# The last down projection with its tokens on the partitions

## The reference

```python
def squared_relu_mlp(h, w1, w2):
    return jnp.square(jax.nn.relu(h @ w1)) @ w2
...
        x = x + squared_relu_mlp(rms_norm_2(x, norm_mlp[layer]), mlp_w1[layer], mlp_w2[layer])
...
    return rms_norm_2(x, final_norm)
```

## Time and profile before

| what | us |
|---|---|
| median of three runs | 1201.18 |
| the three runs | 1198.7, 1201.18, 1201.41 |
| profiled execution, span from first to last instruction | 1197.3 |
| PE busy | 1187.6 (99%) |
| VectorE busy | 867.8 (72%) |
| ScalarE busy | 646.7 (54%) |
| GpSimd busy | 220.6 (18%) |

### The profile page before, as it was taken

One profiled execution on the slowest core, in us unless ns is written; L12 is line 12 of the kernel. 1 busy time (PEld: TensorE's weight loads), 2 busy tenths in 40 slices (PEclk: granted clock), 3 DMA queues, 4 the chain that ended last, 5 costly groups with the idle time before them and its releaser, 6 DMA issues.

```text
span 1197.3 us, 19531 instructions
## 1 busy us (share of the span) xinstructions
PE 1187.6 (99%) x7802; PEld 1060.7 (89%) x7802; DVE 867.8 (72%) x1199; ACT 646.7 (54%) x868; POOL 220.6 (18%) x110
## 2 busy tenths in 40 slices
PE   9999999999999999999999999999999999999997
PEld 6888889988899888888999988888899878888886
DVE  6877767788868877766788786655579777766553
ACT  6655554465654755545643555543446784555441
POOL 0443301000000344310000025510000340554000
PEclk9999999999999999999999999999999999999999
DMA  8655555953345555555545555555576305555540
GB/s 315 213 178 195 191 177 182 285 201 107 106 150 181 179 204 179 200 186 189 177 160 179 193 199 203 179 206 177 192 265 246 107 2 178 209 181 205 179 174 36
DMA packets 31569, 217.53 MB, mean 182 GB/s; under 512 B 3584, under 2 KB 3856, under 8 KB 6272
## 3 DMA queue, kind: packets, MB, share of 16 engines
q1 hardware_dynamic: 30000, 210.33, 50.4%
q0 software_dynamic: 1344, 5.53, 1.6%
q10 hardware_dynamic: 144, 0.52, 0.1%
HBM read 215.30 MB, written 4.22 MB: 183 GB/s over the span
## 4 chain that ended last, share of the span: by engine, by line
PE 96%; DVE 2%; ACT 1%; DMA 1%; issue 0%; POOL 0%; DVEq 0%; ACTq 0%; SPq 0%; POOLq 0%
PE bank L1564 42%; PE bank L1565 21%; PE bank L1557 8%; PE bank L1558 7%; PE bank L1559 7%; PE bank L1965 1%; PE bank L1673 1%; DVE w_hl L816 1%; PE bank L1737 1%; PE bank L1675 1%; PE bank L1674 1%; DMA raw<-weights 1%; ACT w_hl L418 0%; PE bank L1859 0%; PE bank L1842 0%; PE bank L1878 0%
## 5 line engine op out<-in xcount | busy, mean ns | idle before, releaser
L816 DVE TENSOR_TENSOR w_hl<-raw,w_hl 128x2048 fp32r<-128x2048 f32 x194 | 444.1, 2289 | 116.5 <-ACT w_hl L418 115.5
L418 ACT ACTIVATE w_hl<-raw 128x2048 fp32r<-128x2048 f32 x195 | 370.6, 1903 | 113.8 <-PE bank L1565 65.5
L1564 PE MATMUL bank<-x_hl,w_hl 128*128 128x512 f32 x908 | 316.5, 395 | 0.0
L1564 PE MATMUL bank<-hidden,w_hl 128*128 128x512 f32 x832 | 288.6, 394 | 0.0
L369 POOL TENSOR_TENSOR hidden<-hid_f,hidden 128x256 fp32r<-128x256 f32 (+1 forms) x76 | 189.5, 2493 | 519.8 <-ACT hidden L501 307.0
L1565 PE MATMUL bank<-x_hl,w_hl 128*128 128x256 f32 x908 | 251.9, 277 | 0.0
L1565 PE MATMUL bank<-hidden,w_hl 128*128 128x256 f32 x832 | 230.5, 277 | 0.0
L1564 PEld LDWEIGHTS bank<-x_hl,w_hl 128*128 128x128 f32 x908 | 170.3, 188 | 39.6
L1564 PEld LDWEIGHTS bank<-hidden,w_hl 128*128 128x128 f32 x832 | 156.0, 188 | 36.2
L1565 PEld LDWEIGHTS bank<-x_hl,w_hl 128*128 128x128 f32 x908 | 170.6, 188 | 0.1
L479 ACT ACTIVATE second<-bank 128x512 f32<-128x512 f32 (+1 forms) x107 | 57.2, 535 | 199.1 <-PE bank L1565 199.0
(11 more groups left out here) (385 smaller groups left out, 1536.0 us busy)
## 6 DMA issues: line engine op xcount, KB each, us to landing
raw<-weights SPq DMA_DIRECT2D x197, 1024.0 KB, 4.9
bias_skew<-bias_rows POOLq DMA_DIRECT2D x1, 3072.0 KB, 26.0
gate_or_bias<-bias_skew POOLq DMA_DIRECT2D x1, 2048.0 KB, 9.6
h<-x_t SPq DMA_DIRECT2D x2, 512.0 KB, 6.0
out_t<-out_g SPq DMA_DIRECT2D x4, 256.0 KB, 2.5
con<-consts SPq DMA_DIRECT2D x1, 769.5 KB, 13.3
raw<-weights ACTq DMA_DIRECT2D x1, 512.0 KB, 5.2
raw<-weights SPq DMA_DIRECT2D x1, 512.0 KB, 7.9
```

What stands on the lines that cost most here:

```text
L418: nc.scalar.activation(dst, src, ACT.Copy).then_inc(hi_split, 1)
L816: V.tensor_tensor(w_lo[:, s, :], raw[:, s, :], w_hi[:, s, :].bitcast(F32), ALU.subtract).then_inc(lo_split, 1)
L1564: mm(out_, w_hi[:, s, c:c + m], x, start=start, stop=False, **kw)
```

## The change

The down projection of "mlp1" is turned round. Its weights are packed as 2 x 8 chunks, each 512 hidden features by half of the 1024 output columns (`HALF`), and a new `last_down` takes the place of the second part of `feed_forward` on PE: for each half, chunk and tile of 128 tokens, four hidden tiles of 128 tokens are stationary in turn and 512 columns of weights move. The sums of a half lie in two banks, one per token tile (6 and 7, then 0 and 1). In the last half the final two chunks are taken for all of the first token tile before the second. Behind the first chunk PE transposes `h` (16 pieces) into banks 0 to 3 and `t_b` (two) into bank 4; ScalarE copies `h` out as `h_tok`, VectorE the factor as `r_tok`.

The rest then works on token rows: one VectorE operation per bank updates `h_tok`; ScalarE squares it and sums along the row in the same instruction; the mean, Ln, Exp and Newton step are taken per token tile; the factor is a scalar of each partition. The final gain, before a column of `par`, is loaded by GpSimd's queue into all partitions (`gain_b`, in place of `sv`). GpSimd multiplies three of the four quarters by the gain and the whole first token tile by its factor, VectorE and ScalarE take one half of the second tile each. Three stores leave from SP, SP and ScalarE, as rows of `out`, and the host no longer transposes. The matmuls against ones and zeros and the spreading of the factors at the end go. Cut to its core:

```diff
-            downs("mlp1", "final", None)
+            last_down()
...
+                nxt(c0)
+                act.wait_ge(tok_mm, 1)
+                for n in range(4):
+                    nc.scalar.activation(half_of(h_tok[:, n // 2, :], n % 2), bank[:, n, :], ACT.Copy).then_inc(tok_in, 1)
+                for i in range(1, FC):
+                    nxt(c0 + i)
...
+                    nc.scalar.activation(sq_flat[:, HALF * n:HALF * n + HALF], half_of(h_tok[:, n % 2, :], n // 2), ACT.Square,
+                                         accum_out=f_ss[:, n:n + 1]).then_inc(f_sq, 1)
...
+                y = half_of(out_g[:, 1, :], 0)
+                nc.scalar.activation(y, y, ACT.Copy, scale=f_r[:, 1:2]).then_inc(y_act, 1)
+                act.wait_ge(y_act, 1)
+                act.dma_start(out[P:2 * P, 0:HALF], y).then_inc(stored, 16)
...
+                V.scalar_tensor_tensor(out=hj, in0=bank[:, LAST_BANKS[half] + t, :], scalar=r_tok[:, 0, t:t + 1], in1=hj,
+                                       op0=ALU.mult, op1=ALU.add).then_inc(f_upd, 1)
...
+            dve.wait_ge(f_r_ready, 2)
+            V.tensor_scalar(y, y, f_r[:, 1:2], None, ALU.mult).then_inc(y_dve, 1)
...
+                order = [(half, i, t) for half in range(2) for i in range(FC - 2 * half) for t in range(2)]
+                order += [(1, i, t) for t in range(2) for i in (FC - 2, FC - 1)]
...
+                        mm(o, a, wh, start=f == 0, stop=False)
+                        mm(o, a, wl, start=False, stop=False)
+                        ins = mm(o, l, wh, start=False, stop=f == 2 * MF - 1)
...
+                        pe.wait_ge(ab_ready, b + MF)
+                        pe.wait_ge(h_upd, UPD["mlp1"])
+                        for n in range(2):
+                            for k in range(KT):
+                                nc.tensor.transpose(bank[:, 2 * n + k // 4, k % 4 * P:k % 4 * P + P], h[:, k, P * n:P * n + P], ident)
...
+            pool.wait_ge(phi_mm, 1)
+            pool.dma_start(gain_b, last_gain.partition_broadcast(P)).then_inc(last_gain_in, 16)
             low("mlp1")
...
+            pool.wait_ge(f_r_ready, 1)
+            nc.gpsimd.tensor_tensor(out_g[:, 0, :], out_g[:, 0, :], f_r[:, 0:1].to_broadcast([P, D]),
+                                    ALU.mult).then_inc(y_pool, 1)
```

More of the change, by code:

```diff
@@ L140, in done, with program @@
         self.wait()
-def program(nc, x_t, p_t, positions, weights, small, consts, rel_bias, bias_rows, bias_skew, out):
+def program(nc, x_t, p_t, positions, weights, small, consts, rel_bias, last_gain, bias_rows, bias_skew, out):
     with ExitStack() as ctx:
@@ L528, in downs @@
                     if used and o == KT - 1:
                         nxt(c)
[L530 to L539, removed]
+                rsqrt(following, load=stage in ("ffn1", "ffn2"))
@@ L955, in downs @@
                     if ended:
[L956 to L963, removed]
+                        dve.wait_ge(second_out, SECOND[stage] + UPS[stage] + o + 1)
+                        st.done(V.tensor_tensor(t_ab[:, 0, :], bank[:, DOWN_BANKS[o], 0:S], second[:, o % 2, 0, :], ALU.add))
+                        st.done(V.tensor_tensor(t_ab[:, 1, :], t_ab[:, 0, :], factor_of[:, :], ALU.mult))
                         V.scalar_tensor_tensor(out=h[:, o, :], in0=t_ab[:, 1, :], scalar=scale, in1=h[:, o, :],
@@ L1533, in _ @@
             factor("mlp1")
-            st.done(V.tensor_tensor(t_b[:, :], r_sb[:, :], r_sb[:, :], ALU.mult))
+            V.tensor_tensor(t_b[:, :], r_sb[:, :], r_sb[:, :], ALU.mult).then_inc(r_ready, 1)
+            dve.wait_ge(r_ready, 3)
             ups("mlp1")
-            downs("mlp1", 1.0, "final", None, None)
-            dve.wait_ge(ss_ready, NO["final"] + 1)
-            V.tensor_scalar(f_ms, bank[:, SUMS, 0:2], 1.0 / D, EPS, ALU.mult, ALU.add).then_inc(ms_ready, 1)
-            dve.wait_ge(r0_ready, NO["final"] + 1)
@@ L1540, in _ @@
[L1540 to L1548 removed]
+            c0 = C["mlp1"] + MF
@@ new lines, in _ @@
+            dve.wait_ge(r2_in, 1)
+            dve.wait_ge(tok_in, 4)
+            for n in range(2):
+                last_update(n)
+            dve.wait_ge(f_sq, 2)
+            st.done(V.tensor_scalar(f_ss[:, 0:2], f_ss[:, 0:2], EPS * D, None, ALU.add))
+            for i in range(FC, 2 * FC):
+                nxt(c0 + i)
+            last_update(2)
+            mean_of(0)
+            root_of(0)
+            last_update(3)
+            dve.wait_ge(last_gain_in, 16)
+            dve.wait_ge(f_upd, 4)
@@ L2299, in pack_weights @@
     pairs(w["b_w_o_2"][0].reshape(16, 64, D)[NSA_ORDER].reshape(D, D))
-    mlp(w["mlp_w1_2"][1], w["mlp_w2_2"][1])
+    mlp(w["mlp_w1_2"][1])
+    for half in range(2):
+        for i in range(FC):
+            add(rows(w["mlp_w2_2"][1][512 * i:512 * i + 512, HALF * half:HALF * half + HALF]))
     out = np.stack(chunks)
```

169 lines of the change are left out of this document (108 added, 61 removed).

## The result

The changed kernel takes 1207.26 us in the median of six runs (1203.73 to 1209.89), the kernel before 1199.21 on the same chips (1197.99 to 1201.41): ratio 1.0058, 95% interval 1.0043 to 1.0072. By this ratio it is 7 us slower, by the two medians 8, where 2.55 us less was forecast.

A forecast was written before the change was run, and what follows sets the result against it. PE was taken to bound the kernel, with 96% of the chain of waits. Matmuls -1.76, transposes +2.06 and tail -2.85 gave -2.55 us, taken over to the median of 1201.18: 1198.6 us, range 1196.6 to 1201.4.

The forecast's parts named there:

- the clock's: Rival, last down projection's second chunk: clock falls behind the transposes; 48 matmuls at the 1.2 GHz level give 1208.8 us; chance 0.04.
- Matmuls: Last down projection: 384 matmuls of 512 columns at 0.2276 us, 87.40 us instead of 89.16, giving 1.76 us back.
- the cheap end: Rival, last projection and tail: 0.2266 us per matmul, cheaper rows, stores that do not meet; 1197.7 us; chance 0.18.
- Transposes: Behind the last projection's first chunk: 18 new transposes on PE, no wait ahead, costing 2.06 us.
- The change of halves: Between the last projection's two halves: weight splits are ready with 4.9 us of cover, so PE does not wait; cost 0.
- The tail: From the last matmul's end to the span's end: 6.85 us instead of 9.7, giving 2.85 us back.

The follow-up runs named there:

- pad_t: Run pad once more, timed: the changed kernel with eight unused columns in the table of gains; 1196.12 us, median of 10, ratio 0.9976 to the kernel before.
- pad: The changed kernel with eight unused columns where the final norm's gains stood in the table of gains, so every SBUF tile lies as before; 1195.01 us.
- sbpad: The changed kernel with 32 unused bytes per partition behind the table of gains in SBUF alone, the DRAM table as the change has it; 1199.37 us.
- conlow: The changed kernel with 32 unused bytes behind the tile con, so con alone lies 32 bytes lower than before the change; 1199.19 us.
- switch: Run pad with an added multiplication of ones by ones ahead of the two output projections at 365 and 671 us; 1198.81 us.

## Why the prediction was wrong

**The step that failed** is the ground under the sum: a term that I put at nothing without a reason. I set the sum on the profiled span of 1197.3 and on a projection that starts at 1098.28, and so took it as given that 1098 us of untouched code would take as long as before. They took 10.9 more, because the change moved `ones` and with it left the pairs of `wide` at 353.3 ns where they had run at 346.7. Nothing that I costed or bounded reached there; of the rivals only the clock's was of the right size, and for another reason. I knew that the final gains leave `par`; that nine tiles are allocated behind `par`, and what this moves, I didn't ask. No row of the trace of before tells that a place could matter, but that the pairs have two paces could be read there: 353 ns from 365 to 393 us, 347 behind it.

A second fault is smaller and lies in the base. The forecast of 1198.6 us carries over 3.9 us from the span to the median of three runs. In all later runs the time lies only 1.7 to 2.1 us above the run's own span, and the kernel before came to 1199.21 in six runs: the base of 1201.18 was 2 us too high. Set on 1199.21, the same sum gives 1196.7, and run pad_t, the change without the shift, measured 1196.12.

The Trainium skill (SBUF — State Buffer, "Operand start alignment") asks of an operand's start only that it be a multiple of its element size, and adds that this is about legality, not speed. All five places of `ones` are multiples of 16 bytes and legal by it; between them the runs show more than 10 us.

**The terms themselves**, from the changed kernel's trace:

- *Matmuls.* From 1116.85 to 1198.02 the last 358 of the 384 follow each other at 0.2267 us (81.17 / 358), 0.2276 was predicted and 0.2266 given as the cheap end. Over 384 that is 0.35 us less. The mean of the earlier trace rows holds nine first steps of 0.224 to 0.236; the others there are 0.226 or 0.227.
- *Transposes.* From 1114.42 to 1116.85 are 2.43 us, two ordinary steps are in that: 1.98 us for all 18, against 2.06, with no wait ahead.
- *The clock.* The rival had it fall behind the transposes. The two stretches behind them and the middle of the projection, by stretch (columns as in the earlier trace rows):

```profile
1113.00:1118.00 5.00, 5.00 (x32) 4.39 (x32) 2.32 (x2) 3.10 (x4) 2.26 (x1) 1.00 0.53 180
1118.00:1128.00 10.00, 10.00 (x46) 8.27 (x45) 3.45 (x3) 3.07 (x4) 0.00 (x0) 1.00 0.38 129
1140.00:1160.00 20.00, 20.00 (x90) 16.57 (x89) 10.00 (x6) 6.41 (x5) 0.02 (x1) 1.00 0.52 192
```

  1.00 throughout, as the earlier trace rows had it. The Trainium skill ("TensorE: Matmul & The Clock Gate", Part 4) says that a transpose does not count as PE-busy in the same way as other matmuls; 18 of them in 1.98 us did not lower the clock, nor did the longest series in the trace of before, 20 in the attention from 950.9 to 953.3 us (granted clock 1.00).
- *The change of halves.* PE has no idle time ahead of any matmul of the projection, as said.
- *The tail.* 6.6 us against 6.85. The path is the one predicted: update 0.75, square 0.63, mean to Newton, one output step, stores. ScalarE's store leaves 3.71 behind the last matmul (3.75 predicted), and the span ends 2.9 later (3.1). GpSimd's multiplication of the first tile ends 0.55 ahead of the last matmul's end (0.6 predicted), and its store is issued at 1197.88, still ahead of it.

**The sum without the shift** was tried as run pad_t. Its span is 1193.7: the projection from 1097.92 (0.36 earlier than before), 89.23 us to the end of its last matmul at 1187.15, and 6.57 of tail. Where 2.55 us were forecast, stage and tail give back 0.09 + 3.15 = 3.2, and the timed ratio of 0.9976 is 2.9 us of 1199.38, with an interval of 1.2 to 4.4. The last rows of its tail:

```profile
1186.76 0.39 PE L1814 MATMUL bank<-w_hl,hidden 128*128 128x512 f32 x1
1187.18 0.75 DVE L1584 SCALAR_TENSOR_TENSOR h_tok<-bank,r_tok,h_tok 128x512 f32<-128x512 f32 x1 [2.63 <-PE bank L1814]
...
1190.85 0.35 ACTq L581 DMA_DIRECT2D out_t<-out_g  x1
```

So the mechanism of the changed stage and the tail held, and each size was within 0.4 us; the change with eight unused columns beats the kernel before, the change as it stands loses to it.

## What to carry to other kernels

Before reading the changed stage of a trace, compare where it starts: if that has moved, code that was not edited has, and the means of its largest groups show which, even by 4 ns. A change that takes a tile or a few columns away moves all that is allocated behind it; leave the gap open, as run pad does, when the question is what the edit itself is worth, and try the place of small tiles as a parameter of its own when a stream of matmuls fills the span.

## What the runs showed of the hardware that I had not expected

A stream of pairs of 512 and 256 columns without idle time, at a granted clock of 1.00, has two rhythms, 347 and 353 ns a pair, each kept for hundreds of pairs; in three of the eight traces that began fast behind the first sum (sbpad, conlow, switch) it tipped into the slow one at a wait for weights, 48 pairs on; 256-column triples (0.120 us each) and 512-column matmuls with the weights moving (0.2267) showed one. Behind triples the pairs began slow in every run. A matmul that sums with `ones` in between brought the fast rhythm with that tile at byte 219888 or 219904 of a partition and left the slow one with it at 219872, 219936 or 219968: 1195 to 1200 us against 1206 to 1215 (medians or single executions), runs of both kernels among each.
